# Forming three of every four blocks of the MLP's first matrix product from seven block products instead of eight

## The chip, the cores and the metric

The kernel runs on one NeuronCore of one Trainium2 chip. The metric is the device time of one execution in microseconds (us), lower is better. Three runs of the kernel before gave 1271.30, 1271.11 and 1271.58 us, so the median is 1271.3 us.

## What is computed

A two-layer encoder over 528 tokens (16 learned meta tokens and 512 inputs) with 1024 features. Layer 0 is an mLSTM mixer, layer 1 a differential attention; each is followed by a squared-ReLU MLP. Only the two MLPs change. Cut to what matters, the reference has:

```
def sq_relu_mlp(y, w_up, w_down):          # w_up 1024 x 4096, w_down 4096 x 1024
    u = y @ w_up
    return jnp.square(jax.nn.relu(u)) @ w_down

h = h + sq_relu_mlp(rmsnorm(h, norm_gains[i, 1]), mlp_w_up[i], mlp_w_down[i])
```

Layer 0 computes all 528 tokens, layer 1's MLP only the 512 that are put out.

## The kernel before

**Layout.** Features lie on the 128 partitions and tokens along the free axis: `h`, `yh`, `yl`, `ah`, `al` are tiles of 8 feature blocks by 528 tokens. Every matrix product is done in fp32r with a high and a low part of each side: `x = xh + xl`, and the product is `wh*yh + wh*yl + wl*yh`, three matmuls in place of one. ScalarE makes the high part by a copy that rounds (`wh<-raw`, line 513), VectorE the low part by a subtraction (`wl<-raw,wh`, line 885).

**Units.** The MLP works in units of 128 output features. A unit multiplies a 1024x128 strip of weights with all tokens: 8 blocks of the contraction times 3 matmuls times the token spans. In layer 0 there are two spans of 264 tokens (48 matmuls of 264 columns a unit), in layer 1 one of 512 (24 matmuls of 512 columns). Two neighbouring units share one DMA of weights (1 MB) and are called a row pair here. A group is 8 units of the first matrix ("up", 4 row pairs) and then 8 units of the second ("down", 4 row pairs) that use the 8 activation blocks just made; each layer has 4 groups, so 16 up pairs and 16 down pairs. Groups 1 to 3 run in loops of the engines' own.

**Around a unit.** After an up unit VectorE takes the positive part out of PSUM and multiplies by the token's norm factor (`tbuf<-ps,rb`, line 1105). ScalarE squares it twice: in full precision into `abuf` (line 708) and rounded into `ah` (line 709). VectorE makes `al<-abuf,ah` (line 1110). A down unit starts with block 0 of `ah`/`al` and waits, block by block, for `a_ready` (which `al` counts up). After a down unit VectorE adds PSUM to `h` (line 1083). SyncE issues the weight DMAs into two raw slots, each as soon as both units in a slot are split. GpSimd has nothing in the MLP but the masks for layer 1's attention (`qm`, `khm`, lines 499 and 500), which PE's first score products (line 1531) wait for.

**What sets the order.** Each engine has one queue in program order; semaphores tie them together. On VectorE an iteration of an up unit is: split a later unit's weights, then lines 1105 and 1110. PE's unit waits for its weights (`split_lo`) and for its PSUM banks (`evac`). The few lines on which the rest hangs:

```
for kb in range(kb0, kb1):
    ...
    for n, (w, m) in enumerate(((wh, mh), (wh, ml), (wl, mh))):
        for s, (t0, w_) in enumerate(spans):
            last = mm(ps[:, bank + s, 0:w_], w[:, slot, kb, :], m[:, kb, t0:t0 + w_],
```

## Time and profile before

| | before |
|---|---|
| median of 3 runs | 1271.3 us |
| the profiled execution's own time | 1271.11 us |
| its span, first to last instruction | 1269.4 us |
| granted TensorE clock, mean | 0.995 of 2.4 GHz |
| PE busy | 1239.7 us (98%), 8261 matmuls |
| VectorE busy | 696.9 us (55%) |
| ScalarE busy | 574.3 us (45%) |

Busy time of PE is the union of overlapping matmuls, whose ends are modelled; how long one really takes is read from start to start. An engine's idle time costs nothing unless another one waits for what it does next. The profiled execution took 1271.11 us, 1.7 us more than its span.

### The profile page before, as it was taken

What the parts mean: (1) busy time and instruction counts of PE and PEld (TensorE: products, weight loads), DVE (VectorE), ACT (ScalarE), POOL (GpSimd) and SP (SyncE); (2) the same over time, 40 slices, a digit from 0 to 9 for tenths busy, and PEclk for the clock granted to TensorE, in tenths of its full rate; (3) what the DMA queues carried; (4) which work ended last, traced back from release to release, by engine and by line L of the source; (5) the groups of instructions that cost most, each with busy time, mean ns of one, the idle gap of its engine ahead of it and who ended that gap; (6) DMA issues with size and microseconds to landing.
All of it is one profiled execution on the core that took longest, in us unless ns stands there. A gap on an engine that the chain in (4) does not pass through costs nothing.

```text
span 1269.4 us, 20753 instructions
## 1 busy us (share of the span) xinstructions
PE 1239.7 (98%) x8261; PEld 1137.4 (90%) x8261; DVE 696.9 (55%) x1026; ACT 574.3 (45%) x975; POOL 65.6 (5%) x105
## 2 busy tenths in 40 slices
PE   7999999999999999999999999998999999999997
PEld 6999999999999999999998998886788888888886
DVE  5778777754334334334558888785543442443443
ACT  4676776533224124123346787775431231331342
POOL 4121120110000000000010000000000000000000
PEclk9899999999999999999999999999999999999998
DMA  6433332222233222322222122212333322223311
GB/s 161 105 91 95 83 98 77 87 85 88 84 96 100 86 81 99 98 67 99 83 67 84 51 66 66 83 34 70 97 100 100 100 100 91 74 99 99 100 67 67
DMA packets 141575, 110.29 MB, mean 87 GB/s; under 512 B 22104, under 2 KB 139920, under 8 KB 141520
## 3 DMA queue, kind: packets, MB, share of 16 engines
q1 hardware_dynamic: 140000, 104.93, 27.0%
q0 software_dynamic: 1392, 4.49, 1.4%
q8 instruction: 39, 0.64, 0.2%
q14 instruction: 16, 0.13, 0.0%
q10 hardware_dynamic: 128, 0.09, 0.0%
HBM read 107.38 MB, written 2.13 MB: 86 GB/s over the span
## 4 chain that ended last, share of the span: by engine, by line
PE 76%; issue 18%; DVE 2%; ACT 2%; POOL 1%; DMA 1%; SPq 0%; DVEq 0%; POOLq 0%; ACTq 0%
PE ps L1313 72%; PE ps L1363 1%; PE ps L1381 1%; DMA raw<-in_mlstm_w_in_dram 1%; ACT wh L513 0%; PE ps L1404 0%; DVE wl L885 0%; PE ps L1416 0%; PE ps L1437 0%; PE ps L1470 0%; PE ps L1329 0%; POOL acc L430 0%; DVE fin L1295 0%; DVE yl L927 0%; POOL sql L506 0%
## 5 line engine op out<-in xcount | busy, mean ns | idle before, releaser
L1313 PE MATMUL ps<-yh,wh 128*128 128x264 f32 (+1 forms) x1472 | 366.5, 312 | 0.0
L1313 PE MATMUL ps<-yl,wh 128*128 128x264 f32 (+1 forms) x1472 | 361.9, 309 | 0.0
L1313 PE MATMUL ps<-yh,wl 128*128 128x264 f32 (+1 forms) x1472 | 360.9, 309 | 0.0
L513 ACT ACTIVATE wh<-raw 128x1024 fp32r<-128x1024 f32 x192 | 200.3, 1050 | 185.5 <-PE ps L1313 184.7
L1313 PE MATMUL ps<-ah,wh 128*128 128x264 f32 (+1 forms) x960 | 257.4, 322 | 1.6 <-DVE al L1284 0.8
L1313 PE MATMUL ps<-al,wh 128*128 128x264 f32 (+1 forms) x960 | 257.1, 322 | 0.0
L1313 PE MATMUL ps<-ah,wl 128*128 128x264 f32 (+1 forms) x960 | 256.4, 321 | 0.0
L1313 PEld LDWEIGHTS ps<-yh,wh 128*128 128x128 f32 x1472 | 240.2, 189 | 14.1 <-issue 0.2
L1313 PEld LDWEIGHTS ps<-yh,wl 128*128 128x128 f32 x1472 | 239.3, 189 | 13.8
L885 DVE TENSOR_TENSOR wl<-raw,wh 128x1024 fp32r<-128x1024 f32 x192 | 236.7, 1233 | 26.7 <-ACT wh L513 23.7
L1313 PEld LDWEIGHTS ps<-yl,wh 128*128 128x128 f32 x1472 | 239.3, 189 | 12.9 <-issue 0.2
L1313 PEld LDWEIGHTS ps<-ah,wh 128*128 128x128 f32 x960 | 159.7, 188 | 17.1 <-DVE al L1284 1.2
L1083 DVE TENSOR_TENSOR h<-ps,h 128x528 f32<-128x528 f32 (+1 forms) x80 | 55.9, 699 | 212.0 <-PE ps L1313 212.0
L1313 PEld LDWEIGHTS ps<-ah,wl 128*128 128x128 f32 x960 | 159.4, 188 | 13.7
L1313 PEld LDWEIGHTS ps<-al,wh 128*128 128x128 f32 x960 | 159.4, 188 | 13.3
L708 ACT ACTIVATE abuf<-tbuf 128x528 f32<-128x528 f32 (+1 forms) x64 | 40.9, 638 | 267.3 <-DVEq L1108 267.3
L1105 DVE SCALAR_TENSOR_TENSOR tbuf<-ps,rb 128x528 f32<-128x528 f32 (+1 forms) x64 | 44.8, 700 | 113.0 <-PE ps L1313 107.3
L1110 DVE TENSOR_TENSOR al<-abuf,ah 128x528 fp32r<-128x528 f32 (+1 forms) x64 | 44.8, 701 | 82.6 <-ACT ah L709 82.6
L513 ACT ACTIVATE yh<-h,gains 128x528 fp32r<-128x528 f32 (+1 forms) x32 | 23.4, 730 | 60.9 <-DVEq L1088 55.2
L709 ACT ACTIVATE ah<-tbuf 128x528 fp32r<-128x528 f32 (+1 forms) x64 | 39.9, 623 | 0.0
L759 ACT ACTIVATE e<-ps,stat 128x272 f32<-128x272 f32 (+3 forms) x48 | 26.5, 556 | 19.9 <-DVE stat L1168 18.4
L460 POOL TENSOR_SCALAR_AFFINE_SELECT dmat<-dmat 128x128 f32<-128x128 f32 (+1 forms) x40 | 19.2, 512 | 138.4 <-ACT dmat L587 138.4
(220 smaller groups left out, 1068.9 us busy)
## 6 DMA issues: line engine op xcount, KB each, us to landing
raw<-in_mlp_w_up_dram SPq DMA_DIRECT2D x32, 1024.0 KB, 5.3
raw<-in_mlp_w_down_dram SPq DMA_DIRECT2D x32, 1024.0 KB, 4.9
raw<-in_diff_w_in_dram SPq DMA_DIRECT2D x24, 512.0 KB, 3.7
raw<-in_mlstm_w_in_dram SPq DMA_DIRECT2D x16, 512.0 KB, 4.2
raw<-in_mlstm_w_in_dram SPq DMA_DIRECT2D x16, 256.0 KB, 5.4
raw<-in_mlstm_w_out_dram SPq DMA_DIRECT2D x3, 1024.0 KB, 5.0
raw<-in_diff_w_out_dram SPq DMA_DIRECT2D x3, 1024.0 KB, 4.9
mbc<-gate_rows POOLq DMA_DIRECT2D x8, 264.0 KB, 5.4
```

The source lines that it names most:

```text
L460: last = nc.gpsimd.affine_select(out=blk, in_=blk, compare_op=ALU.is_ge, fill=0.0, base=0, pattern=[[1, w]], channel_multiplier=-1)
L513: return nc.scalar.activation(o, i, ACT.Copy, scale=scale)
L708: nc.scalar.activation(abuf[:, t0:T], tbuf[:, t0:T], ACT.Square).then_inc(sqa_done, 1)
L709: nc.scalar.activation(ah[:, k, t0:T], tbuf[:, t0:T], ACT.Square).then_inc(ah_done, 1)
L759: nc.scalar.activation(dst, src, ACT.Exp, bias=stat[:, i % 2, c:c + 1], accum_out=stat[:, i % 2, 2 + c:3 + c]).then_inc(exp_done[c], 1)
L885: V.tensor_tensor(wl[:, k, :, :], raw[:, k // 2, :, P * (k % 2):P * (k % 2) + P], wh[:, k, :, :].bitcast(F32), ALU.subtract).then_inc(spli ...
L1083: ins = V.tensor_tensor(tokens(h[:, b, :], spans), src or banks(k, spans), tokens(h[:, b, :], spans), ALU.add)
L1105: V.scalar_tensor_tensor(tokens(tbuf[:, :], spans), banks(k, spans), 0.0, tokens(rb[:, :], spans), ALU.max, ALU.mult).then_inc(evac, 1)
L1110: V.tensor_tensor(al[:, k, t0:T], abuf[:, t0:T], ah[:, k, t0:T].bitcast(F32), ALU.subtract).then_inc(a_ready, 1)
L1313: last = mm(ps[:, bank + s, 0:w_], w[:, slot, kb, :], m[:, kb, t0:t0 + w_], start=(kb == 0 and n == 0), stop=(kb == CB - 1 and n == 2))
L1363: last = mm(ps[:, b, c:c + t1 - t0], what(rows, j), p, start=(b not in seen), stop=(n in (1, len(PIECES) - 1) and i == len(passes) - 1))
L1381: last = mm(ps[0:rows, b, c:c + t1 - t0], ks[par][:, s0:s0 + rows], q[:, t0:t1], start=(m == 0), stop=(m == 1))
```

## The change

In groups 1 to 3 of each layer every up pair is computed by block products after Winograd's form of Strassen's scheme; group 0's four up pairs and all down pairs stay as they were (called plain). For such a pair ("crossed" in the code) the weights are a 2x2 of blocks: two halves of the contraction (512 rows each) by two units (128 columns each). The tokens are two halves: 264 and 264 in layer 0, 256 and 256 in layer 1. Eight half-size products become seven, named A11, A12, S2, S3, S1, S4, A22. Each is 4 blocks of the contraction times 3 matmuls: 12 matmuls of 264 or 256 columns. What is added for it:

- VectorE makes four combined weight blocks (`form`: S1, S3, S2, S4, each 512 columns wide, into `lof`), and the low parts of all seven (`form_lo`, `natural_lo`). ScalarE makes the high parts.
- VectorE adds the products up in seven steps (`total`: C11, U2, U3, C22, U4, C12, C21), each 264 or 256 columns with one operand in PSUM. ScalarE copies A11 out of PSUM first (`snap`).
- The norm factor can't be put on afterwards, so the normed input itself is made once a layer: `scaled_y` (8 operations), `y_forms` (4 combined inputs, 8 operations), `forms_lo` (4 of 4x264 columns) and `scaled_lo` (4 of 2x528), with ScalarE's `forms_hi` and `scaled_hi`. They stand in the queues at up pairs 0 to 3 and at pair 4.
- The positive part squared is made in one VectorE pass (`square`: max(x,0) times x), and ScalarE only copies it into `ah`. Plain pairs keep two squares on ScalarE.
- All MLP loops are written out. Weights lie in two halves of SBUF, one a pair; the masks on GpSimd and VectorE move from before layer 0's MLP to its last down pairs and its end.

Cut to its core (`i` is the pair, 0 to 31 in a layer; `m` the unit in it; `after` is true if pair i+2 is crossed):

```diff
+            def total(i, name):
...
+                    if name == "C11":
+                        dve.wait_ge(m_done, items + DONE[i, "A12"])
+                        dve.wait_ge(t1_done, ranks + RANK[i])
...
+                        o, x, y = tb[0][:, first], t1[:, 0:w], p("A12")
...
+                    V.tensor_tensor(o, x, y, ALU.add).then_inc(c_done, 1)
...
+                def square(i, m):
...
+                    V.scalar_tensor_tensor(ab[m][:, t0:T], tb[m][:, t0:T], 0.0, tb[m][:, t0:T], ALU.max, ALU.mult).then_inc(m_relu, 1)
...
+                def form(i, name, after):
...
+                    a11, a12, a21, a22 = r[:, 0:4, 0:P], r[:, 4:8, 0:P], r[:, 0:4, P:2 * P], r[:, 4:8, P:2 * P]
...
+                    x, y, op = {"S1": (a21, a22, ALU.add), "S3": (a11, a21, ALU.subtract),
+                                "S2": (f[:, 16:20, :], a11, ALU.subtract), "S4": (a12, f[:, 8:12, :], ALU.subtract)}[name]
...
+                    dve.wait_ge(m_done, items + last_use(i, name))
+                    V.tensor_tensor(f[:, out_rows, :], x, y, op).then_inc(s_made, 1)
...
+                for i in range(PAIRS):
...
+                    if crossed(i - 1):
+                        total(i - 1, "C21")
+                    elif i > 0:
+                        evacuate(i - 1, 1)
+                    if crossed(i - 1):
+                        act_lo(i - 1, 0)
+                    if crossed(i + 1):
+                        form_lo(i + 1, "S23")
+                    if crossed(i - 1):
+                        square(i - 1, 1)
+                    if crossed(i):
+                        total(i, "C11")
+                    if crossed(i + 1):
+                        form_lo(i + 1, "S14")
+                    if crossed(i):
+                        total(i, "U2")
+                    if is_up(i - 1):
+                        act_lo(i - 1, 1)
+                    if crossed(i + 1):
+                        natural_lo(i + 1, False)
+                    elif 1 <= i < PAIRS - 1:
+                        plain_lo(layer, i + 1, 1)
+                    if crossed(i):
+                        total(i, "U3")
...
+                    if not crossed(i):
+                        evacuate(i, 0)
+                        if is_up(i):
+                            if i < 2:
+                                scaled_y(4 * i)
+                            act_lo(i, 0)
+                            if i == 2:
+                                for n in range(4):
+                                    y_forms(n)
+                            if i == 3:
+                                for n in range(4):
+                                    forms_lo(n)
...
+                    after = crossed(i + 2)
+                    if after:
+                        natural_lo(i + 2, True)
+                    elif i + 2 < PAIRS:
+                        plain_lo(layer, i + 2, 0)
...
+                    if crossed(i):
+                        total(i, "C22")
+                        total(i, "U4")
+                    if after:
+                        form(i + 2, "S1", 0)
+                        form(i + 2, "S3", 0)
+                    if crossed(i):
+                        total(i, "C12")
+                    if after:
+                        form(i + 2, "S2", 1)
+                    if crossed(i):
+                        square(i, 0)
+                    if after:
+                        form(i + 2, "S4", 3)
...
+                def plain(i, m):
...
+                        if not is_up(i) and i % 8 == 4 and m == 0:
+                            pe.wait_ge(a_ready, 8 * (4 * layer + i // 8) + kb + 1)
...
+                def product(i, name):
+
+                    n = 7 * (i % 8) + PRODUCTS.index(name)
+                    bank = n % 8
...
+                    if n >= 8:
+
+                        last, product_ = i - i % 8 + (n - 8) // 7, PRODUCTS[(n - 8) % 7]
+                        if product_ == "A11":
+                            pe.wait_ge(t1_done, ranks + RANK[last])
+                        else:
+                            pe.wait_ge(c_done, 7 * ranks + summed(last, FREED[product_]))
...
+                        for n, (x, y) in enumerate(((hi, mh), (hi, ml), (lo, mh))):
+                            last = mm(ps[:, bank, 0:w], x[1 - i % 2][:, row + kb, :], y,
+                                      start=(kb == 0 and n == 0), stop=(kb == 3 and n == 2))
```

PE before, at an up unit of layer 0 in the groups' loop; `wh`, `wl` are the weights' parts, `yh`, `yl` the input's, and each row is two matmuls with the same weights on the two halves of the tokens:

```order
L1313 MATMUL ps<-yh,wh 128x264 x2
L1313 MATMUL ps<-yl,wh 128x264 x2
L1313 MATMUL ps<-yh,wl 128x264 x2
L1305 REGISTER_ALU
L1313 MATMUL ps<-yh,wh 128x264 x2
```

PE now, at product S2 of the second crossed pair (pair 9 of layer 0); `hi`, `lo` are the weights' parts, `th`, `tl` those of the combined input:

```order
L1947 MATMUL ps<-yh,lo_107 128x264
L1947 MATMUL ps<-th,hi_106 128x264 [waits c_done,m_lo]
L1947 MATMUL ps<-tl,hi_106 128x264
L1947 MATMUL ps<-th,lo_107 128x264
L1947 MATMUL ps<-th,hi_106 128x264
```

A matmul now stands alone on its weights, no longer in twos, and a product waits for the sum that frees its bank (`c_done`) besides its weights (`m_lo`).

VectorE before, for one up unit (layer 0's first and second):

```order
L885 TENSOR_TENSOR wl<-raw,wh 128x1024 [waits split_hi]
L1105 SCALAR_TENSOR_TENSOR tbuf<-ps,rb 128x528 [waits unit_done,rb_ready]
L1110 TENSOR_TENSOR al<-abuf,ah 128x528 [waits evac,ah_done]
L885 TENSOR_TENSOR wl<-raw,wh 128x1024 [waits split_hi]
L1105 SCALAR_TENSOR_TENSOR tbuf<-ps,rb 128x528 [waits unit_done]
L1110 TENSOR_TENSOR al<-abuf,ah 128x528 [waits evac,ah_done]
```

VectorE now, from C21 of pair 8 (the first row) to U3 of pair 9 and the next pair's weights; `u`, `t` and `tbuf` hold the sums, `lof` the combined weights:

```order
L1375 TENSOR_TENSOR tbuf_115<-u_113,ps 128x264 [waits c_done,m_done]
L1387 TENSOR_TENSOR al<-abuf,ah 128x528 [waits ah_done]
L1327 TENSOR_TENSOR lo_110<-lof_111,hi_109 128x1024 [waits m_hi,s_made]
L1381 SCALAR_TENSOR_TENSOR abuf_116<-tbuf_115 128x528 [waits ah_done,c_done]
L1375 TENSOR_TENSOR tbuf<-t_117,ps 128x264 [waits ah_done,m_relu,t1_done,m_done]
L1327 TENSOR_TENSOR lo_110<-lof_111,hi_109 128x1024 [waits m_hi,s_made]
L1375 TENSOR_TENSOR u_112<-t_117,ps 128x264 [waits c_done,m_done]
L1387 TENSOR_TENSOR al<-abuf_116,ah 128x528 [waits ah_done]
L1334 TENSOR_TENSOR lo_110<-raw,hi_109 128x512 [waits m_hi]
L1375 TENSOR_TENSOR u_113<-u_112,ps 128x264 [waits c_done,m_done]
L1334 TENSOR_TENSOR lo_107<-raw,hi_106 128x1024 [waits m_hi]
```

In place of 6 operations for a pair VectorE now has 20, the sums taken in between the making of the next two pairs' weights.

VectorE now, behind the evacuation of pair 2's first unit up to the last activation block of group 0 (`tf` are the combined inputs, `tl` their low parts, `tbuf<-ps,rb` the evacuations of units (2,1), (3,0) and (3,1)):

```order
L1436 TENSOR_TENSOR tf<-yn_121,tf 128x528
L1287 TENSOR_TENSOR lo_110<-raw,hi_109 128x1024 [waits m_hi]
L1397 SCALAR_TENSOR_TENSOR tbuf_115<-ps,rb 128x528 [waits ah_done,m_done]
L1387 TENSOR_TENSOR al<-abuf_116,ah 128x528 [waits ah_done]
L1287 TENSOR_TENSOR lo_110<-raw,hi_109 128x1024 [waits m_hi]
L1397 SCALAR_TENSOR_TENSOR tbuf<-ps,rb 128x528 [waits ah_done,m_done]
L1387 TENSOR_TENSOR al<-abuf,ah 128x528 [waits ah_done]
L1449 TENSOR_TENSOR tl<-tf,th 128x1056 [waits t_made,th_done] x4
L1287 TENSOR_TENSOR lo_107<-raw,hi_106 128x1024 [waits m_hi]
L1397 SCALAR_TENSOR_TENSOR tbuf_115<-ps,rb 128x528 [waits ah_done,m_done]
L1387 TENSOR_TENSOR al<-abuf_116,ah 128x528 [waits ah_done]
```

Eight operations on `tf` (the last is shown) and four on `tl` now stand ahead of the evacuations in VectorE's queue, where before each unit had its own three alone.

## Rows read from the trace of the kernel before

**Rows 1.** The page: span and busy engines.

```profile
span 1269.4 us, 20753 instructions
PE 1239.7 (98%) x8261; PEld 1137.4 (90%) x8261; DVE 696.9 (55%) x1026; ACT 574.3 (45%) x975; POOL 65.6 (5%) x105
```

**Rows 2.** The chain, in order of time (start us, us, what): both MLPs.

```profile
274.56 370.04 PE ps L1313 x3024
...
906.31 322.49 PE ps L1313 x1392
```

**Rows 3.** Windows in the two MLPs: us, busy (x count), PEclk, DMA share, GB/s.

```profile
278.00:635.00 357.00, 357.00 (x2920) 357.00 (x2920) 145.60 (x165) 104.57 (x136) 0.00 (x0) 1.00 0.28 90
910.00:1225.00 315.00, 315.00 (x1362) 255.36 (x1361) 129.63 (x148) 94.13 (x123) 0.00 (x0) 1.00 0.29 95
```

**Rows 4.** Timeline of PE in an mLSTM head (start us, us, what).

```profile
102.22 0.28 PE L1363 MATMUL ps<-phi,vh 128*128 128x256 f32 x1
102.34 0.28 PE L1363 MATMUL ps<-plo,vh 128*128 128x256 f32 x1
...
102.57 0.23 PE L1363 MATMUL ps<-phi,vh 128*128 128x128 f32 x1
...
103.57 0.33 PE L1363 MATMUL ps<-phi,vh 128*128 128x272 f32 x1
103.74 0.29 PE L1363 MATMUL ps<-plo,vh 128*128 128x272 f32 x1
```

**Rows 5.** Weight loads, by line of the page.

```profile
L1313 PEld LDWEIGHTS ps<-yh,wh 128*128 128x128 f32 x1472 | 240.2, 189 | 14.1 <-issue 0.2
```

**Rows 6.** Timeline of VectorE in an mLSTM head.

```profile
114.99 0.42 DVE L1046 SCALAR_TENSOR_TENSOR acc<-acc,ps 128x256 f32<-128x256 f32 x1 [0.33 <-PE ps L1416]
115.33 0.43 DVE L1048 SCALAR_TENSOR_TENSOR acc<-acc,ps 128x272 f32<-128x272 f32 x1
115.68 1.22 DVE L885 TENSOR_TENSOR wl<-raw,wh 128x1024 fp32r<-128x1024 f32 x1
116.81 0.70 DVE L1056 SCALAR_TENSOR_TENSOR acc<-acc,of 128x528 f32<-128x528 f32 x1
117.92 0.71 DVE L904 TENSOR_TENSOR of<-ps,rb 128x528 f32<-128x528 f32 x1 [0.40 <-PE ps L1313]
118.54 0.70 DVE L1066 TENSOR_TENSOR nf<-nf,acc 128x528 f32<-128x528 f32 x1
119.24 0.69 DVE L1070 TENSOR_TENSOR vl<-ps,vh 128x512 fp32r<-128x512 f32 x1
119.84 0.27 DVE L1072 TENSOR_TENSOR vl<-ps,vh 16x128 fp32r<-16x128 f32 x1
```

**Rows 7.** Timeline of VectorE at an up unit of layer 0, then layer 1.

```profile
280.47 0.71 DVE L1105 SCALAR_TENSOR_TENSOR tbuf<-ps,rb 128x528 f32<-128x528 f32 x1 [0.27 <-PE ps L1313]
282.49 0.71 DVE L1110 TENSOR_TENSOR al<-abuf,ah 128x528 fp32r<-128x528 f32 x1 [1.31 <-ACT ah L709]
283.44 1.23 DVE L885 TENSOR_TENSOR wl<-raw,wh 128x1024 fp32r<-128x1024 f32 x1 [0.24 <-ACT wh L513]
...
907.73 0.69 DVE L1105 SCALAR_TENSOR_TENSOR tbuf<-ps,rb 128x512 f32<-128x512 f32 x1 [3.57 <-ACT rb L551]
909.70 0.69 DVE L1110 TENSOR_TENSOR al<-abuf,ah 128x512 fp32r<-128x512 f32 x1 [1.28 <-ACT ah L709]
```

**Rows 8.** Timeline of ScalarE at the same up unit of layer 0.

```profile
281.82 0.63 ACT L709 ACTIVATE ah<-tbuf 128x528 fp32r<-128x528 f32 x1
282.36 1.04 ACT L513 ACTIVATE wh<-raw 128x1024 fp32r<-128x1024 f32 x1
```

**Rows 9.** Activations' blocks, and what PE's down units waited, by line of the page.

```profile
L1313 PE MATMUL ps<-ah,wh 128*128 128x264 f32 (+1 forms) x960 | 257.4, 322 | 1.6 <-DVE al L1284 0.8
```

**Rows 10.** Timelines of GpSimd and PE: masks, and the first score products.

```profile
646.45 1.10 POOL L500 CAST khm<-kmask 64x528 fp32r<-64x528 f32 x1
...
663.66 0.30 PE L1531 MATMUL ps<-khm,qm 128*128 128x144 f32 x1 [0.89 <-DVE vf L904]
```

More of the change, by code:

```diff
@@ L61, with is_up, crossed, pe_order @@
 AHEAD = 2
-MISSED = [(7, 6), (14, 12)]
 CAME = [(0, 0, 0), (9, 9, 8)]
-U_IN0, U_OUT0, U_MLP0 = 0, 24, 32
-U_IN1, U_OUT1, U_MLP1 = 96, 120, 128
-U_END = 192
+U_IN0, U_OUT0 = 0, 24
+U_IN1, U_OUT1 = 32, 56
+U_END = 64
+PLAIN = 8
+PAIRS = 8 * GROUPS
+def is_up(i):
+    return 0 <= i < PAIRS and i % 8 < 4
+def crossed(i):
+    return is_up(i) and i >= PLAIN
+PRODUCTS = ("A11", "A12", "S2", "S3", "S1", "S4", "A22")
+def pe_order():
+    for i in range(PAIRS):
+        yield from [(i, e) for e in (PRODUCTS if crossed(i) else (0, 1))]
+def counted(things):
+    return {x: n + 1 for n, x in enumerate(things)}
+DONE = counted(pe_order())
+READY = counted((i, e) for i in range(PAIRS) for e in (("A1", "S23", "S14", "A22") if crossed(i) else (0, 1)))
+PLAINS = counted((i, m) for i in range(PAIRS) if not crossed(i) for m in range(2))
+RANK = counted(i for i in range(PAIRS) if crossed(i))
+N_DONE, N_READY, N_PLAIN, N_CROSSED = (len(x) for x in (DONE, READY, PLAINS, RANK))
+SUMS = {"C11": 1, "U2": 2, "U3": 3, "C22": 4, "U4": 5, "C12": 6, "C21": 7}
+FREED = {"A12": "C11", "S2": "U2", "S3": "U3", "S1": "U4", "S4": "C12", "A22": "C21"}
+SLOT = {"A11": 0, "A12": 1, "S2": 2, "S3": 3, "S1": 4, "S4": 5, "A22": 6}
+FORM = {"S1": 0, "S2": 1, "S3": 2, "A22": 3}
+UP_BANKS = [(0, 2, 4, 6, 0, 2, 4, 6), (4, 5, 7, 6, 4, 5, 7, 6)]
+def bank_of(i, name):
+    return (7 * (i % 8) + PRODUCTS.index(name)) % 8
+def summed(i, sum_):
+    return 7 * (RANK[i] - 1) + SUMS[sum_]
 ALL = [(0, HALF), (HALF, HALF)]
@@ L392, in _ @@
             out_weights(w_out0, U_OUT0)
-            mlp(0, U_MLP0)
-            with sp.Fori(0, HEADS) as i:
+            mlp(0)
+            for j in range(3):
+                sp.wait_ge(m_lo, READY[PAIRS - 2 + j // 2, 1])
+                sp.dma_start(raw[:, j // 2, :, P * (j % 2):P * (j % 2) + P], columns(w_in1, D * j, P)).then_inc(unit_in[j], 16)
+            with sp.Fori(1, HEADS) as i:
                 for j in range(3):
@@ L1151, in _ @@
             dve.wait_ge(lam_dve, 4)
+            mlp(0, ALL)
+            split(U_IN1 + 2, 2)
             dve.wait_ge(mask_base, 3)
@@ L1490, in _ @@
                 blocks(U_OUT0 + k, k % 4, ah, al, ALL, 2 * (k % 4), U_OUT0 + k - 3)
-            def mlp(layer, base, spans):
-                g0 = 4 * layer
-                def group(u0, g, first=False):
-                    for k in range(8):
-                        unit(u0 + k, k, yh, yl, spans, y_block(2 * layer + 1) if first and k == 0 else None)
-                        if first and k == 0:
-                            mean_squares(2 * layer + 1, spans)
-                    for k in range(8):
-                        unit(u0 + (8 + k), k, ah, al, spans,
-                             (lambda kb: pe.wait_ge(a_ready, g * 8 + (kb + 1))) if k == 0 else None)
-                group(base, g0, True)
-                with pe.Fori(1, GROUPS - layer) as g:
-                    group(g * 16 + base, g + g0)
```

478 lines of the change are left out of this document (366 added, 112 removed).

## The prediction

> **What bounds the kernel now.** I read the page first: PE is busy 98% of the span, VectorE 55%, ScalarE 45% [rows 1]. Then the chain in order of time: each MLP is one unbroken piece on PE, 3024 matmuls in 370.04 us in layer 0 and 1392 in 322.49 us in layer 1 [rows 2]. So a matmul of 264 columns takes 0.1224 us from start to start and one of 512 columns 0.2317 us. The windows confirm that no one else sets the pace there: PE fills 357.00 of 357.00 us and 315.00 of 315.00 us at clock 1.00 (the 2.4 GHz level), VectorE is busy 145.60 and 129.63 us, ScalarE less [rows 3]. In the MLPs, then, time is matmuls times their spacing, and whatever is added on VectorE costs nothing until PE waits for it.
>
> **What the change takes from PE.** Layer 0: a crossed pair goes from 2 units x 48 = 96 matmuls to 7 x 12 = 84, all of 264 columns. 12 matmuls x 0.1224 = 1.469 us a pair, 12 pairs: **17.6 us**. Layer 1: 48 matmuls of 512 columns become 84 of 256. For these I need the spacing of 256-column matmuls with their own weights each; four starts in an mLSTM head, 102.22, 102.34, (102.45) and 102.57, give 0.35 us for three, 0.117 us [rows 4]. 48 x 0.2317 = 11.12 us against 84 x 0.1175 = 9.87 us, 1.25 us a pair, 12 pairs: **15.0 us**. Bounds: the spacing can't be above that of 264 columns with equal loads (0.1224: 10.1 us gained) unless the weight load shows, and 0.117 gives 15.5. Together 32.6 us (27.7 to 33.1). Down pairs, heads and DMA bytes stay the same.
>
> **What it adds on VectorE.** Durations are one thing, spacing another: after a 528-column operation at 117.92 the next starts at 118.54, 0.62 us later though the first lasts 0.71; 512 columns 0.60, 272 columns 0.35, 256 columns 0.34, 1024 columns 1.13 [rows 6]. The order now shows 20 operations a crossed pair: 7 sums (0.34), 2 squares and 2 `al` (0.62), 4 forms and one half split (0.60), 3 of 1024 columns (1.13): 2.4 + 2.5 + 3.0 + 3.4 = **11.3 us** against PE's 84 x 0.1224 = 10.28 (9.87 in layer 1). For these pairs VectorE is the longer one. But only pairs 8 and 9 of a group carry all of it: pair 10 makes no further forms (8.9 us), pair 11 neither and splits plain weights (7.2 us). Walked through the queue: VectorE enters pair 8 some 1.3 us late (form S4 of pair 9 must wait until unit (7,1) has let go of its weights), is 2.4 to 2.7 us late after pair 8, about 3.7 after pair 9 at the most, about 2.3 after pair 10, and has caught up within pair 11.
>
> Is this lateness covered? A product waits for the sum that frees its bank eight products back: S2 of pair 9 for C11 of pair 8, which is due a whole pair, 9.9 to 10.3 us, earlier. The weights of pair i+1 are split in pair i, 7 us or more ahead of use. So 3.7 us is hidden by PE's own next pair. If that cover is gone, each us beyond it is paid once a group. The next in line is the end of pair 11: `al` of the last block. From A22's end: 0.05 to start, C21 0.34, `al` of block 6 0.62, square 0.71, ScalarE's copy 0.63 (its length by the `ah` row, [rows 8]) with two hand-overs of 0.04, `al` 0.71: 3.1 to 3.2 us. PE's down unit comes to its block 7 after 7 x 6 x 0.1224 = 5.14 us (layer 1: 7 x 3 x 0.2317 = 4.87). 1.7 us to spare, nothing paid. ScalarE has 3 x 1.04 + 2 x 0.63 and, by the same slope, about 0.6 and 0.4 for the half copy and A11: 5.4 us a pair, no limit.
>
> **Where I expect a wait: pair 3 to pair 4 of group 0.** Eight y-forms and four `tl` operations stand ahead of evacuations there, and each evacuation needs its round through ScalarE. VectorE's queue from the evacuation of (2,0): evacuation to `al` 2.0 (282.49 - 280.47, [rows 7]), `al` 0.62, y-forms 8 x 0.62 + 0.1, split 1.13, evacuation (2,1) to `al` 2.0, `al` to the split behind ScalarE's copy 0.95 (283.44 - 282.49), split 1.13, evacuation (3,0) to `al` 2.0, 0.98 to the first `tl`, 4 x 1.17, split 1.13, evacuation (3,1) to `al` 2.0, `al` and hand-over 0.75: 24.4 us. PE in the same time: three units of 5.87 us and 5.14 us up to block 7, less 0.05: 22.7. **1.7 us** of wait. Layer 1: 4 x 1.97 + 0.60 + 4.9 + 3 x 1.13 + 2 x 0.95 + 4 x 1.13 + 0.73 = 23.9 against 3 x 5.56 + 4.87 - 0.05 = 21.5: **2.4 us**. Together 4.1 us (0 if VectorE catches up earlier, up to 8 if each hand-over takes 0.1 more). Before, all the waits of PE's down units came to 1.6 us [rows 9], so this one is new. `scaled_lo` at pair 4 (4 x 1.17) comes after it and PE needs it only at pair 8.
>
> **At nothing.** The masks: 0.8 us on VectorE and eight copies of up to 1.1 us on GpSimd now begin about 5.5 us after layer 0's MLP ends, done at most 14 us after it; the first score product came 19 us after that end (663.66 against 644.6, [rows 10, 2]). SyncE's waits are those of two splits ago, as before; each load has over half a pair of time. The written-out loops: the unbroken piece of layer 0 holds the unlooped first group and the looped ones alike, at one spacing [rows 2].
>
> **Sum.** 1271.1 (this execution's time) - 32.6 + 4.1 = **1242.6 us**. The median of the runs shown lies 0.2 above that execution, which changes nothing. PE's waits end in a clock question only if they get long; I take the clock as it is.
>
> **Rivals.**
>
> 1. *All hidden*: no wait at pair 4, because VectorE starts evacuations earlier than in my walk. 1271.1 - 32.6 = 1238.5. For it: 1.7 and 2.4 us are differences of sums of 24. Against: the walk leaves nothing idle on VectorE but the rounds through ScalarE.
>
> 2. *VectorE's operations don't overlap*, each takes its whole duration: 0.43, 0.71, 0.69 and 1.23 [rows 6, 7] make 13.0 us a pair, and VectorE is 1.3 + 2 x 2.7 = 6.7 us late after two pairs, 4.7 at the end of pair 11 (10.2 and 8.3 us of work in the last two). `al` of block 7 comes 3.1 + 4.7 = 7.8 us into the down unit: 2.7 us a group, in layer 1 some 4.1; six groups 20.4, the y-chain 2.2 more: 1265. Half of it gives 1254. For it: 20 operations with two or three waits each, many on the operation shortly before. Against: the rows just quoted, where an operation starts 0.09 before the last ends. The Trainium skill, "VectorE: DVE Perf Modes", section "The DRAIN you can't avoid", says that the next operation does not start until the pipe is empty. By that rule this rival would be the forecast; the trace disagrees for operations that don't wait (0.62 spacing at 0.71 duration).
>
> 3. *Slower, by VectorE as the bound*: if besides full durations each of the 20 operations waits 0.1 us for its partner, a group's four pairs take 44.4 + 8 = 52.4 us on VectorE against 41.1 on PE; with 1.3 late at the start and 2.0 to spare that is 10.6 us a group, 64 in all: 1306. It turns the gain into a loss from 4.8 us a group on, that is at 46.6 us of work in four pairs, against 38.7 at spacings. Against: the waits are mostly for things long done.
>
> 4. *Slower, by weight loads that show*: each 256-column matmul brings its own load, whose row shows 0.189 us [rows 5]. In an mLSTM head a 272-column matmul behind narrow ones took 0.17 us (103.57 to 103.74, [rows 4]). If all 84 did: 14.3 us a pair, 2.5 and 3.2 us more than before, 12 pairs each: 68 + 4 = 1343. It loses from 0.132 us a matmul on in layer 1. Against: at 264 columns the same load is there for every matmul, at 0.1224. The Trainium skill, "TensorE: Matmul & The Clock Gate", section "Part 3: Packing small matmuls", lets a load overlap running matmuls only when the row group differs; the 0.117 of the rows at 256 columns disagrees with it.
>
> **How the numbers follow.** My forecast (1239.5 to 1247) 0.55; all hidden 0.14; VectorE's lateness partly or wholly paid (1247 to 1265) 0.25; slower by VectorE 0.04; slower by loads 0.02. The range of 8 in 10 takes in the first two and rival 2 to a bit over its half: 1238 to 1257. 0.2% of 1271 is 2.5 us, about what can be told from no change here. Faster 0.94, same 0.01, slower 0.05.
>
> **What the new profile would show.** PE 8261 - 4608 + 4896 = 8549 matmuls; 1008 of them of 264 columns and 1008 of 256 in products, at 0.122 and 0.1175; VectorE busy some 200 us more (24 x 6.6 and two y-chains of about 20), the 20 operations a pair at 11 to 12 us; PE waiting at `ps<-ah,hi` for `al` once a layer at pair 4, about 2 us, and not at pairs 12, 20, 28. Wrong if waits stand at each group's first down pair (rival 2), inside pairs 9 to 11 for `c_done` (rival 3), or if the 256-column spacing is over 0.125 (rival 4).

## The result, and the profile after

The changed kernel takes 1242.75 us (median of 4 executions, 1241.34 to 1244.20); the kernel before took 1271.23 us on the same chip. The ratio is 0.9776, 95% interval 0.9759 to 0.9793. The forecast was 1242.6 us, the range 1238 to 1257. The profiled execution was the longest of the four, 1244.20 us, with a span of 1242.1 us, 27.3 us shorter than before.

The page of the changed kernel (compare [rows 1]: 8549 matmuls, as forecast, and 190 us more on VectorE, where some 200 were forecast):

```profile
span 1242.1 us, 21698 instructions
PE 1208.6 (97%) x8549; PEld 1129.8 (91%) x8549; DVE 887.2 (71%) x1386; ACT 608.2 (49%) x1015; POOL 62.0 (5%) x105
L1911 PE MATMUL ps<-ah,hi 128*128 128x264 f32 (+1 forms) x768 | 206.2, 323 | 3.8 <-DVE al L1387 3.8
```

The last row answers to [rows 9]: PE's waits for activation blocks rose from 1.6 to 3.8 us. L1911 is the line of plain matmuls now, L1947 that of the block products. The chain of the changed kernel in order of time (start us, us, what) answers to [rows 2]:

```profile
322.57 41.92 PE ps L1911 x342
364.49 40.77 PE ps L1947 x336
405.25 46.76 PE ps L1911 x384
452.01 40.77 PE ps L1947 x336
...
976.43 39.69 PE ps L1947 x336
1016.12 44.63 PE ps L1911 x192
```

The single unbroken piece of each MLP is now cut at product lines, with no idle time between the pieces shown. Four crossed pairs take 40.77 us in layer 0 (0.1213 us a matmul of 264 columns) and 39.69 us in layer 1 (0.1181 us of 256). In layer 0 they took 384 x 0.1224 = 47.0 us before, in layer 1 192 x 0.2317 = 44.5 us: 6.2 and 4.8 us less a group, three groups each. Four plain pairs take 46.76 us (0.24 less than before) and 44.63 us (0.14 more).

The piece of layer 0 is broken once, at pair 4 of group 0, and that of layer 1 at the same place. Timeline of PE there in the changed kernel (start us, us, what, and in brackets the idle time and its releaser):

```profile
320.50 0.40 PE L1911 MATMUL ps<-ah,lo 128*128 128x264 f32 x2
322.57 0.51 PE L1911 MATMUL ps<-ah,hi 128*128 128x264 f32 x2 [1.66 <-DVE al L1387]
...
932.26 0.39 PE L1911 MATMUL ps<-ah,lo 128*128 128x512 f32 x1
934.84 0.50 PE L1911 MATMUL ps<-ah,hi 128*128 128x512 f32 x1 [2.18 <-DVE al L1387]
...
935.98 0.63 PE L1911 MATMUL ps<-al,hi 128*128 128x512 f32 x1
936.40 0.63 PE L1911 MATMUL ps<-ah,lo 128*128 128x512 f32 x1
```

From start to start PE stood 1.8 us beyond the usual spacing in layer 0, and 2.3 us in layer 1. Behind the second wait something else is to be seen: soon the matmuls lie 0.42 us apart (935.98 to 936.40) instead of 0.233. The windows of the changed kernel around both waits say why (us, busy and count of PE, PEld, DVE, ACT, POOL, then PEclk, DMA share, GB/s):

```profile
316.00:326.00 10.00, 8.34 (x69) 8.13 (x68) 8.52 (x10) 7.29 (x9) 0.00 (x0) 1.00 0.08 18
932.00:942.00 10.00, 7.82 (x27) 5.89 (x26) 8.53 (x10) 6.83 (x8) 0.00 (x0) 0.83 0.31 105
```

The granted clock is 1.00 around the first wait and 0.83 around the second: about a third of those 10 us was granted at half speed, 1.2 GHz. Those are 3.4 us, and they cost half of that, 1.7 us.

So the account of the two spans is: block products 18.7 + 14.4 = 33.1 gained, plain pairs 20 x 0.06 - 20 x 0.035 = 0.5 gained, waits 4.1 and clock 1.7 lost. That leaves 27.8 gained where 27.3 is measured.

### The profile page after: what moved, and what is told of

It is laid out like the page before. It is cut to its first block, busy times and chain, and to the rows that moved or that the text cites. A ratio compares the mean times of both kernels' runs of the same rounds, so it can differ in the third digit from the quotient of the medians.

```text
span 1242.1 us, 21698 instructions
## 1 busy us (share of the span) xinstructions
PE 1208.6 (97%) x8549; PEld 1129.8 (91%) x8549; DVE 887.2 (71%) x1386; ACT 608.2 (49%) x1015; POOL 62.0 (5%) x105
## 4 chain that ended last, share of the span: by engine, by line
PE 72%; issue 19%; DVE 6%; ACT 3%; POOL 1%; DMA 0%; DVEq 0%; POOLq 0%; ACTq 0%
PE ps L1911 33%; PE ps L1947 19%; PE ps L1691 15%; PE ps L1741 1%; PE ps L1759 1%; DVE wl L1079 1%; DVE tf L1436 1%; ACT wh L627 0%; DVE tbuf L1397 0%; ACT ah L862 0%; DVE tl L1449 0%; DVE lo L1287 0%; DMA meta_in<-in_meta_tokens_dram 0%; PE ps L1782 0%; DVE yl L1121 0%
## 5 line engine op out<-in xcount | busy, mean ns | idle before, releaser
L1911 PE MATMUL ps<-ah,hi 128*128 128x264 f32 (+1 forms) x768 | 206.2, 323 | 3.8 <-DVE al L1387 3.8
L1911 PE MATMUL ps<-al,hi 128*128 128x264 f32 (+1 forms) x768 | 206.0, 323 | 0.0
L1911 PE MATMUL ps<-ah,lo 128*128 128x264 f32 (+1 forms) x768 | 205.3, 321 | 0.0
L1691 PE MATMUL ps<-yh,wh 128*128 128x264 f32 (+1 forms) x704 | 161.2, 303 | 0.4 <-DVE wl L1079 0.4
L1691 PE MATMUL ps<-yl,wh 128*128 128x264 f32 (+1 forms) x704 | 156.1, 296 | 0.0
L1691 PE MATMUL ps<-yh,wl 128*128 128x264 f32 (+1 forms) x704 | 156.0, 296 | 0.0
L1911 PEld LDWEIGHTS ps<-ah,hi 128*128 128x128 f32 x768 | 127.7, 189 | 15.9 <-DVE al L1387 4.5
L1911 PEld LDWEIGHTS ps<-ah,lo 128*128 128x128 f32 x768 | 127.8, 189 | 11.3
L1911 PEld LDWEIGHTS ps<-al,hi 128*128 128x128 f32 x768 | 127.8, 188 | 11.2
L1691 PEld LDWEIGHTS ps<-yh,wh 128*128 128x128 f32 x704 | 112.4, 190 | 3.0 <-DVE wl L1079 0.7
L1947 PE MATMUL ps<-th,hi 128*128 128x264 f32 (+1 forms) x384 | 108.5, 283 | 0.0
L1947 PE MATMUL ps<-tl,hi 128*128 128x264 f32 (+1 forms) x384 | 108.3, 282 | 0.0
L1947 PE MATMUL ps<-th,lo 128*128 128x264 f32 (+1 forms) x384 | 108.2, 282 | 0.0
L1079 DVE TENSOR_TENSOR wl<-raw,wh 128x1024 fp32r<-128x1024 f32 x64 | 80.5, 1259 | 8.1 <-ACT wh L627 6.2
L1947 PE MATMUL ps<-yh,lo 128*128 128x264 f32 (+1 forms) x288 | 81.3, 282 | 0.0
L1947 PE MATMUL ps<-yh,hi 128*128 128x264 f32 (+1 forms) x288 | 81.3, 282 | 0.0
```

The lines of the kernel that those rows point to most:

```text
L1079: V.tensor_tensor(wl[:, k, :, :], raw[:, k // 2, :, P * (k % 2):P * (k % 2) + P], wh[:, k, :, :].bitcast(F32), ALU.subtract).then_inc(spli ...
L1911: last = mm(ps[:, b + s, 0:cw], x[half][:, 20 * m + kb, :], y[:, kb, c0:c0 + cw], start=(kb == 0 and n == 0), stop=(kb == CB - 1 and n == 2))
L1947: last = mm(ps[:, bank, 0:w], x[1 - i % 2][:, row + kb, :], y, start=(kb == 0 and n == 0), stop=(kb == 3 and n == 2))
```

## Experiments

All are the changed kernel with one edit. An edit ahead of a line moves its number: the plain matmuls are L1911 or L1916 below, `al` L1387 or L1392. Each ratio is to the kernel before on the same chip.

**The changed kernel once more.**

> The changed kernel once more, unchanged, to see whether the half-clock stretch behind layer 1's wait of 2.3 us comes in every execution. If the four times seen so far (1241.3 to 1244.2) differ by whether it came: a profile without it has a span near 1240.4, one with it 1242.1, layer 1's pair 4 taking 13.5 us or 15.2. If it comes always, the spread has another cause.

It took 1243.0 us (1241.24 to 1244.53, 5 executions; ratio 0.9782, 0.9768 to 0.9795). The wait at pair 4 of layer 1 and the 3.4 us at half clock behind it came again at the same place (the two profiled executions, 1244.20 and 1244.28 us, are among the longest, so this doesn't say that every execution has them). A single execution moves by 3 us, and longer ones have a lower mean clock (0.993 at 1244.3 and 1244.5 us, 0.996 at 1241.2), so differences under 2 us are read from the traces below, not from medians.

**The low and high parts of the combined inputs two pairs later.**

ScalarE's part first, then VectorE's, which moves from the up pair 3 to the down pair 5:

```diff
-                    if i == 3:
+                    if i == 5:
                         for n in range(4):
                             forms_hi(n)
...
-                            if i == 3:
-                                for n in range(4):
-                                    forms_lo(n)
...
+                        elif i == 5:
+                            for n in range(4):
+                                forms_lo(n)
```

> The rounding and the low parts of the four combined inputs (forms_hi, forms_lo) move from up pair 3 to down pair 5; nothing else changes. Theory A (the wait of PE at pair 4 is VectorE's queue: 4.7 us of tl operations stand ahead of the last evacuation of group 0): the queue is 4 x 1.17 + 1.0 us shorter, which is more than the 1.9 and 2.3 us waited, so both waits go, and with them the stretch at half clock behind layer 1's: 4.2 + 1.7 us less than the changed kernel, 1237 to 1238.5 us. Theory B (the wait comes from ScalarE's rounds of the evacuations, not from the tl operations in the queue): over 1 us of wait stays at pair 4. Theory C (pair 5's VectorE work then delays a down pair): a new wait at pair 6 or 7 and no gain.

It took 1237.54 us (1237.12 to 1239.74; ratio 0.9745, 0.9731 to 0.9758), 5.2 us below the changed kernel. Its chain in order of time:

```profile
273.72 87.65 PE ps L1911 x720
361.37 40.77 PE ps L1947 x336
...
885.74 83.71 PE ps L1911 x360
969.45 39.69 PE ps L1947 x336
```

Both cuts are gone: 720 and 360 plain matmuls run through without a break. 83.71 / 360 = 0.2325 us, so no part of them ran at half clock either. What was given back is 1.8 + 2.3 + 1.7 = 5.8 us by the trace, 5.2 by the medians. (The spans differ by 6.9 us, 1.2 of it ahead of the first MLP, where this edit isn't.) This ties the wait to the four `tl` operations and their ScalarE partners in front of pair 3's last evacuation; the two were moved together, so their shares aren't told apart. It was put in the forecast as the price of the change; it is the price of the place.

**Half of them later.**

Forms 0 and 1 stay at pair 3, forms 2 and 3 go to pair 5, on ScalarE alike:

```diff
                             if i == 3:
-                                for n in range(4):
+                                for n in range(2):
                                     forms_lo(n)
...
+                        elif i == 5:
+                            for n in range(2, 4):
+                                forms_lo(n)
```

> Only half of these operations (the last two of four, high and low parts) moves to pair 5. Theory A: the queue up to the last activation block of group 0 is 2 x 1.17 us shorter in layer 0 and 2 x 1.14 in layer 1. Layer 0's wait of 1.9 goes wholly, layer 1's 2.3 falls to 0 to 0.2; the clock does not fall. 1237 to 1239 us. Theory B: more than 1 us of the wait stays in each layer.

It took 1237.19 us (1236.88 to 1239.71; ratio 0.9744, 0.9729 to 0.9759), no different from the version above. Layer 0's wait is gone, and 0.08 us of layer 1's is left. These two are the fastest versions of this study, 0.4% below the changed kernel.

**The combined inputs' first eight operations twice.**

```diff
+                        V.tensor_tensor(tf[:, f, o, 0:w], x, y, ALU.subtract).then_inc(pad_done, 1)
+                        padded[0] += 1
+                        dve.wait_ge(pad_done, padded[0])
                         V.tensor_tensor(tf[:, f, o, 0:w], x, y, ALU.subtract).then_inc(t_made, 1)
```

> Each of the eight y-forms at pair 2 is computed twice, each extra one waited for: 8 x 0.73 = 5.8 us more in VectorE's queue in layer 0, 8 x 0.71 = 5.7 in layer 1, nothing on PE. Theory A: nothing of it is hidden, since the queue has no slack left up to pair 4: PE waits 7.7 and 8.0 us there in place of 1.9 and 2.3, and the clock falls to half behind both. 1242.8 + 11.5 + 1.7 to 4 = 1256 to 1258 us. Theory B (VectorE has slack behind pair 2 that the forecast's walk did not see): under 8 us more.

It took 1253.96 us (1253.03 to 1257.09; ratio 0.9873, 0.9858 to 0.9889), 11.2 more. PE's waits in the whole execution, by releaser (us in total, times, longest), begin with:

```profile
PE ps L1915 <- DVE tbuf L1398: 8.0, 2, 4.1
...
PE ps L1915 <- DVE al L1388: 2.9, 2, 1.9
```

Read from start to start the four waits are 4.1 and 2.1 us in layer 0, 4.3 and 1.2 in layer 1: 11.7 in place of 4.1, which is 4 us less than the queue was made longer by. The rest is clock. It fell at three of these waits:

```profile
313.50:316.90 3.40, 3.40 (x18) 3.40 (x17) 2.53 (x3) 1.49 (x3) 0.00 (x0) 0.50 0.05 7
327.10:330.50 3.40, 3.40 (x16) 3.40 (x17) 3.09 (x4) 3.40 (x5) 0.00 (x0) 0.51 0.23 67
931.30:938.10 6.80, 5.68 (x14) 4.51 (x14) 4.11 (x6) 3.90 (x6) 0.00 (x0) 0.50 0.15 50
```

In layer 1 it fell 1.1 us before PE started again (932.42). PE lost some 6.3 us by it in place of 1.7. The longer queue first stops PE at pair 3 for a PSUM bank (`tbuf` frees it), the clock falls behind that wait, and PE comes to the last activation block of group 0 later, so that it waits less there. VectorE's queue from `al` of pair 2's first unit to that block's `al` shows that none of the added work was hidden. First the changed kernel, then this one:

```profile
300.25 0.71 DVE L1387 TENSOR_TENSOR al<-abuf,ah 128x528 fp32r<-128x528 f32 x1 [1.25 <-ACT ah L862]
...
321.81 0.71 DVE L1387 TENSOR_TENSOR al<-abuf,ah 128x528 fp32r<-128x528 f32 x1 [1.24 <-ACT ah L862]
```

```profile
298.75 0.71 DVE L1388 TENSOR_TENSOR al<-abuf,ah 128x528 fp32r<-128x528 f32 x1 [1.25 <-ACT ah L863]
...
326.25 0.71 DVE L1388 TENSOR_TENSOR al<-abuf,ah 128x528 fp32r<-128x528 f32 x1 [1.24 <-ACT ah L863]
```

21.56 us became 27.50: 5.9 more, for eight operations 0.74 apart. PE's start behind the wait for that block is 5.9 us later in layer 0 and 5.8 in layer 1, counted from the start of each MLP's second unit. So each microsecond of queue cost PE one microsecond, part of it as a wait and part as half clock between two waits. Only a half-clock stretch behind the last wait comes on top: layer 0 has one here (327.10) and layer 1 has lost its own. That is why the time is below the 1256 to 1258 us expected, though nothing was hidden.

**One addition more in each crossed pair.**

```diff
+                    for _ in range(1 if name == "U2" else 0):
+                        V.tensor_tensor(o, x, y, ALU.add).then_inc(pad_done, 1)
+                        padded[0] += 1
+                        dve.wait_ge(pad_done, padded[0])
                     V.tensor_tensor(o, x, y, ALU.add).then_inc(c_done, 1)
```

> Every crossed pair gets one addition more on VectorE (the sum U2 is formed twice, one after the other, the second waiting for the first), about 0.45 us a pair, 1.8 us a group of four crossed pairs. Theory (spare time): VectorE's sums of a group may end 1.5 us later before PE waits for the last block's split form in the down pair, and VectorE is 2 us short of PE's time over the four pairs, so 1.8 us a group disappear: 1242 to 1244, no change to the changed kernel. Rival (VectorE has no slack left, since it is the longer one in pairs 8 and 9): each microsecond is paid, 6 groups x 1.8 = 11 us: 1253.

It took 1246.08 us (1244.82 to 1247.48; ratio 0.9801, 0.9785 to 0.9817): 3.3 more than the changed kernel, neither 0 nor 11. The two spans differ by 3.3 us as well. 1.3 of it arose ahead of the first MLP, where this edit isn't: this profile has half clock there that the changed kernel's hasn't (0.72 granted from 21 to 27 us). 0.7 arose elsewhere outside the waits. New waits for `al` make 1.3, from start to start: 0.2 us at the first down pair of each of layer 1's three groups, and 0.6 us at one of layer 0's three groups, the third. So the time to spare was as large as forecast within 0.2 us, and in one group smaller. Why there, the next but one experiment shows.

**Three additions more.** The same edit with `range(3 ...)`.

> The same with three additions more in every crossed pair: 5.4 us a group. Theory (spare time): lateness at the down pair becomes 0.3 + 38.8 + 5.4 - 40.8 = 3.7 us in layer 0 where 1.5 to 1.7 is free, so 2.2 us a group; in layer 1 4.1 against 1.5, 2.6 us a group; 3 x 4.8 = 14.4 us: 1257, and up to 10 more if PE's clock falls behind each of these waits. They stand at each group's first down pair, on PE's line of down products, released by the last `al`. Rival (no slack): 6 x 5.4 = 32 us, 1275, with the waits inside pairs 9 to 11 on VectorE's sums.

It took 1274.59 us (1273.44 to 1276.27; ratio 1.0031, 1.0019 to 1.0042): slower than the kernel before. The size is that of the rival, the place mostly that of the theory. Timeline of PE at a first down pair of layer 0:

```profile
407.71 0.41 PE L1916 MATMUL ps<-ah,lo 128*128 128x264 f32 x2
409.86 0.51 PE L1916 MATMUL ps<-ah,hi 128*128 128x264 f32 x2 [1.74 <-DVE al L1392]
...
411.90 0.51 PE L1916 MATMUL ps<-ah,hi 128*128 128x264 f32 x2 [1.05 <-DVE al L1392]
412.25 0.58 PE L1916 MATMUL ps<-al,hi 128*128 128x264 f32 x2
412.62 0.65 PE L1916 MATMUL ps<-ah,lo 128*128 128x264 f32 x2
```

PE waits for block 6 and again for block 7, 3.1 us together, and then runs at half clock (in the window 412.40 to 415.60 the granted clock is 0.50). Over six groups the waits for `al` come to some 17.6 us. Layer 1's groups add 0.4, 0.4 and 2.5 us at the start of the down pair for the sum that frees a PSUM bank, a wait that the theory didn't have: 20.9 us in all. The MLPs have 23.9 us at half clock in place of 3.4, in 1.8 us of which PE stood still anyway, so the clock costs some 9.3 us more. That makes 30.2 together, where the spans differ by 29.5 and the first MLP began 1.5 us earlier. Two terms of the expectation were short. The lateness at the down pair was 4.5 us, not 3.7: three chained additions take 1.4 us (0.46 each, not 0.45), and VectorE can't use its whole time, as its windows over the last three of the four pairs show in this kernel:

```profile
373.20:383.40 10.20, 10.20 (x86) 10.20 (x86) 9.93 (x18) 4.93 (x7) 0.00 (x0) 1.00 0.15 54
383.40:393.60 10.20, 10.20 (x86) 10.20 (x85) 9.95 (x18) 4.94 (x7) 0.00 (x0) 1.00 0.32 104
393.60:403.80 10.20, 10.20 (x86) 10.20 (x85) 9.55 (x20) 3.47 (x5) 0.00 (x0) 1.00 0.31 105
```

Even 4 us behind, VectorE stands 0.25 to 0.65 us a pair, for its round through ScalarE (`al` waits for `ah` 0.37 us at 399.81). The clock's part, "up to 10", came nearly in full.

**One addition more, and GpSimd's masks one pair later.**

```diff
-            pool.wait_ge(m_done, DONE[PAIRS - 5, "A22"])
+            pool.wait_ge(m_done, DONE[PAIRS - 4, 1])
```

> The kernel with one more addition a crossed pair, and GpSimd's seven mask operations of layer 0 (580.4 to 585.0 us in the changed kernel's trace, at the end of the third group) start one pair later, after the first down pair of the last group. In the changed kernel VectorE's square, `al` and split there take 1.11, 1.01 and 1.62 us in place of 0.71, 0.71 and 1.22. Theory (GpSimd's work beside it slows VectorE by 0.3 to 0.4 us an operation, and so uses up the time to spare in this group alone): PE's wait of 0.64 us at 586.5, seen with one more addition, goes, and the three operations take 0.71, 0.71 and 1.22 again; 0.5 us less than 1246.1. Rival (the third group is late by its own queue): the wait stays where it was.

It took 1245.18 us (1243.57 to 1245.35; ratio 0.9798, 0.9781 to 0.9814). The medians can't tell 0.5 us; the traces can. First the changed kernel at the end of pair 27, where the change has put the masks; the timeline of VectorE:

```profile
581.08 0.71 DVE L1387 TENSOR_TENSOR al<-abuf,ah 128x528 fp32r<-128x528 f32 x1 [0.31 <-ACT ah L627]
581.71 1.11 DVE L1381 SCALAR_TENSOR_TENSOR abuf<-tbuf 128x528 f32<-128x528 f32 x1
583.54 1.01 DVE L1387 TENSOR_TENSOR al<-abuf,ah 128x528 fp32r<-128x528 f32 x1 [0.71 <-ACT ah L627]
584.48 1.62 DVE L1287 TENSOR_TENSOR lo<-raw,hi 128x1024 fp32r<-128x1024 f32 x1
```

and GpSimd in the same time:

```profile
580.84 0.54 POOL L593 MEMSET kmask<- 64x528 f32 x1
581.63 0.63 POOL L598 TENSOR_SCALAR_AFFINE_SELECT qmask<-qmask 64x512 f32<-64x512 f32 x1
...
583.94 1.09 POOL L605 TENSOR_SCALAR_AFFINE_SELECT kmask<-kmask 64x528 f32<-64x528 f32 x1
```

Then VectorE in the kernel with the masks moved, at the same work:

```profile
582.47 0.71 DVE L1392 TENSOR_TENSOR al<-abuf,ah 128x528 fp32r<-128x528 f32 x1 [0.37 <-ACT ah L628]
583.09 0.70 DVE L1386 SCALAR_TENSOR_TENSOR abuf<-tbuf 128x528 f32<-128x528 f32 x1
584.50 0.71 DVE L1392 TENSOR_TENSOR al<-abuf,ah 128x528 fp32r<-128x528 f32 x1 [0.71 <-ACT ah L628]
585.46 1.23 DVE L1288 TENSOR_TENSOR lo<-raw,hi 128x1024 fp32r<-128x1024 f32 x1 [0.25 <-ACT hi L628]
```

The square, `al` and the split take 0.70, 0.71 and 1.23 us again where they took 1.11, 1.01 and 1.62, and PE's wait in the third group is gone. The theory holds: GpSimd's selections, which read and write SBUF, cost VectorE 0.3 to 0.4 us an operation. The `al` of 581.08, for most of its 0.71 us beside GpSimd's memsets (which only write), was not slowed. The Trainium skill, "SBUF — State Buffer", section "Who interferes with whom", says that a VectorE instruction with two SBUF inputs contends with a GpSimd instruction that reads SBUF, not with one that only writes; the trace agrees on both.

**The second square back on ScalarE.**

```diff
-                    V.scalar_tensor_tensor(ab[m][:, t0:T], tb[m][:, t0:T], 0.0, tb[m][:, t0:T], ALU.max, ALU.mult)
+                    V.tensor_scalar(tb[m][:, t0:T], tb[m][:, t0:T], 0.0, None, ALU.max)
-                        copy(ah[:, k, t0:T], ab[m][:, t0:T])
+                        nc.scalar.activation(ab[m][:, t0:T], tb[m][:, t0:T], ACT.Square)
+                        nc.scalar.activation(ah[:, k, t0:T], tb[m][:, t0:T], ACT.Square)
```

> Undoes the change's second part alone: the positive part of a crossed pair's two blocks is taken on VectorE without the square, and ScalarE makes both squares as it does in plain pairs. VectorE does the same count of operations of the same columns, ScalarE 2 x 0.6 us more a pair (6.6 of 10.2 us). One hand-over more lies between the relu and `al` of each block: ScalarE square, then square again, some 0.6 us later. Theory: PE is the bound and the `al` of block 7 then ends 4.3 us into the down pair where 5.14 (4.87) is needed, so no change: 1242 to 1244. Rival: the second square makes `al` late enough to be waited for, 6 x 0.5 to 1 us: 1246 to 1249.

It took 1244.51 us (1244.40 to 1244.84; ratio 0.9793, 0.9776 to 0.9809), 1.8 above the changed kernel's median and within its executions. In its trace PE waits 0.5 us in layer 0's third group and 0.3 us in each of layer 1's three, 1.4 in all. VectorE's single pass is thus worth 1.4 us by the trace. The edit isn't as clean as expected: the positive part alone takes VectorE 0.43 us where the square takes 0.71, and still the group's last `al` ended 4.7 us into the first down pair of layer 0, 1.0 later than in the changed kernel. These are waits for the group's last `al`, so what it shortens is the path from A22 to there; the operations that it leaves to ScalarE are not waited for elsewhere. In this profile the wait of 2.3 us at pair 4 of layer 1 had no half clock behind it.

**Product S2 in narrower matmuls.**

```diff
+                    for c0, cw in ((0, w // 2), (w // 2, w // 2)) if name == "S2" else ((0, w),):
...
-                                mh, ml = th[:, FORM[name], kb, 0:w], tl[:, FORM[name], kb, 0:w]
+                                mh, ml = th[:, FORM[name], kb, c0:c0 + cw], tl[:, FORM[name], kb, c0:c0 + cw]
...
-                            last = mm(ps[:, bank, 0:w], x[1 - i % 2][:, row + kb, :], y,
+                                last = mm(ps[:, bank, c0:c0 + cw], x[1 - i % 2][:, row + kb, :], y,
```

> On PE alone: product S2 of every crossed pair is made in two column halves, 24 matmuls of 132 (layer 1: 128) columns in place of 12 of 264 (256), with the same weights and sums. Theory A (a matmul with its own weights takes what its columns take, down to about 60 ns): no change, 1243. Theory B (the weight load is just hidden at 256 columns and shows below that, 0.109 us or so for the narrow matmuls): 24 x 0.109 - 12 x 0.12 = 1.2 us a pair, 24 pairs, 28 us: 1271. This tells how near the change is to the point at which the loads of its seven products would show.

It took 1272.94 us (1271.57 to 1273.55; ratio 1.0013, 1.0004 to 1.0023): the whole gain of the change is spent. Timeline of PE in a product S2:

```profile
365.68 0.22 PE L1948 MATMUL ps<-th,hi 128*128 128x132 f32 x1
365.74 0.27 PE L1948 MATMUL ps<-tl,hi 128*128 128x132 f32 x1
365.85 0.28 PE L1948 MATMUL ps<-th,lo 128*128 128x132 f32 x1
...
368.08 0.27 PE L1948 MATMUL ps<-tl,hi 128*128 128x132 f32 x1
```

From 365.74 to 368.08 lie 21 matmuls of 132 columns: 0.1115 us each, not 0.060. Half the columns cost 92% of the time. That this is the load and not a fixed price of each matmul is seen at the first narrow one, which took 0.06 us (365.68 to 365.74): beside the matmuls of 264 columns each load had started 0.12 us ahead of its matmul, from here on it is 0.06, and the loads themselves lie 0.11 us apart. The counts of [rows 1] and of the new page say that each matmul had a load of its own before the change too (8261 and 8261, now 8549 and 8549), also where two stand on the same weights. In this kernel's chain four crossed pairs take 45.70 and 44.83 us in place of 40.77 and 39.69, so 3 x 4.93 + 3 x 5.14 = 30.2 us, and 1242.75 + 30.2 is 1272.95. The Trainium skill, "TensorE: Matmul & The Clock Gate", section "LDWEIGHTS (loading the stationary operand)", has a load take its columns divided by 1.2 per ns, 107 ns for 128; the rows' 111.5 is 4% above that.

**The weight store laid out low parts first.**

```diff
-            hi.append(place(f"hi{half}", [P, 28, P], F32R, at, limit))
             lo_at = at[0]
             lo.append(place(f"lo{half}", [P, 28, P], F32R, at, limit))
             lof.append(place(f"lof{half}", [P, 28, P], F32, [lo_at], limit))
+            hi.append(place(f"hi{half}", [P, 28, P], F32R, at, limit))
```

> Only places in SBUF change: in both halves of the weight store the low parts are laid out first and the high parts behind them, in place of high first. Same instructions in the same order. Plain units of 48 matmuls of 264 columns in the changed kernel take 5.824, 5.840, 5.847 and 5.869 us (even pair first and second unit, odd pair first and second), the same in every group, where all took 5.873 before; in layer 1 5.599, 5.596, 5.576 and 5.563. Theory (how fast a weight load follows depends on where in SBUF it lies): the four lengths change by 10 ns or more, the time by 2 us at the most. Rival (it is the neighbourhood in the program, such as waits and semaphore updates between the matmuls): they stay within 3 ns.

It took 1243.37 us (1241.21 to 1245.74; ratio 0.9786, 0.9768 to 0.9804). The lengths of the plain units stayed what they were, 5.818 (5.830 for the first behind crossed pairs; the expectation's 5.824 is their mean), 5.840, 5.847 and 5.869 us in layer 0, within a nanosecond. This theory falls: exchanging the places of high and low parts isn't what sets them. Why 48 equal matmuls take 4 to 55 ns less than the 5.873 us of before, by the unit's place in two pairs and always the same, stays open; it is worth 1.2 us over 20 pairs of layer 0, and 0.7 the other way in layer 1.

## Why the prediction was right, step by step

- *What the change takes from PE.* Right: 32.6 forecast, 33.1 measured. The parts were off in opposite directions by about a microsecond: 264 columns at 0.1213, not 0.1224 (18.7 for 17.6), 256 columns at 0.1181, not 0.1175 (14.4 for 15.0).
- *What it adds on VectorE.* The spacings of [rows 6] were the right durations. (One spacing in them, 118.54 to 119.24 behind a 528-column operation, is 0.70, which the prediction passed over; nothing came of it.) The walk's lateness was up to 1 us too large: C21 of pairs 8, 9, 10 and 11 began 1.4, 2.7, 1.9 and 0.2 us behind the first matmul of the next pair, where 2.4 to 2.7, 3.7, 2.3 and 0 stood. The term at fault is pair 8: the walk had VectorE enter it 1.3 us late and pay the full 20 operations. In the trace it has fewer there (the window counts 15 where pairs 9 and 10 have 18), entered some 0.5 late and twice stood waiting for PE inside it (0.41 us each, before C11 and U3), so up to U3 it wasn't late at all. The changed kernel's VectorE windows over these four pairs show the rest:

```profile
364.32:374.53 10.21, 10.21 (x86) 10.21 (x85) 9.11 (x15) 2.81 (x4) 0.00 (x0) 1.00 0.33 100
374.53:384.70 10.17, 10.17 (x86) 10.17 (x85) 10.00 (x18) 4.94 (x7) 0.00 (x0) 1.00 0.16 46
384.70:394.92 10.22, 10.22 (x87) 10.22 (x85) 10.05 (x18) 4.94 (x7) 0.00 (x0) 1.00 0.21 68
394.92:405.09 10.17, 10.17 (x86) 10.17 (x85) 9.24 (x18) 3.47 (x5) 0.00 (x0) 1.00 0.49 157
```

  In pairs 9 and 10 VectorE is busy 98% and PE never waits: a whole pair of cover hides it.
- *Is this lateness covered?* Yes, with less to spare than forecast. The last `al` of the group, in VectorE's timeline of the changed kernel:

```profile
406.00 0.71 DVE L1387 TENSOR_TENSOR al<-abuf,ah 128x528 fp32r<-128x528 f32 x1 [0.28 <-ACT ah L627]
406.63 0.70 DVE L1381 SCALAR_TENSOR_TENSOR abuf<-tbuf 128x528 f32<-128x528 f32 x1
408.05 0.71 DVE L1387 TENSOR_TENSOR al<-abuf,ah 128x528 fp32r<-128x528 f32 x1 [0.71 <-ACT ah L627]
```

  It ends at 408.76, 3.7 us into the down pair that starts at 405.09; 3.1 to 3.2 was forecast, and 5.14 is needed. What was left out is the 0.2 us from the down pair's first matmul to C21 (A22's last matmul is shown to end 0.17 us into it) and `al` of block 6 waiting 0.28 for its own round. 1.5 us to spare in place of 1.7 to 2.0. The kernels with 1 and 3 additions more measured it: 1.8 us a group nearly vanish, 5.5 us a group cost more than 5.
- *The wait at pair 4.* Right in place, releaser and size: 1.7 and 2.4 forecast, 1.8 and 2.3 measured, and both go when the `tl` operations are moved. Rival 1 is refuted as an account of this kernel; at 1237.5 us it is what the moved version does.
- *"PE's waits end in a clock question only if they get long; I take the clock as it is."* This step failed by 1.7 us: 2.3 us can be long enough. That the total still came out within 0.2 us is luck: 1.7 lost here and 0.5 + 0.5 gained in the products and the plain pairs cancel in part, and the median of four lies 1.5 us below the profiled execution, which was itself 1.6 us above the forecast.
- *At nothing.* True of this kernel, but not because the masks were harmless. The prediction looked only at GpSimd's eight copies behind the MLP. GpSimd's mask operations that now run inside it slow three VectorE operations by 1.1 us together, hidden by the same 1.5 us to spare.
- *Rivals.* Rival 2 (VectorE's whole durations paid) did not happen: no waits at pairs 12, 20 and 28. The section of the Trainium skill that the prediction names there, "VectorE: DVE Perf Modes", "The DRAIN you can't avoid", goes on to say that a next operation that is not held starts earlier. So it doesn't disagree with the rows (0.62 apart at 0.71 us), and by it alone this rival wasn't the forecast. Rival 3, slower by VectorE as the bound, put its turning point at 4.8 us lost a group; three additions more passed it, at 31.8 us over six groups (5.3 each) and 1274.6 us. Rival 4, slower by weight loads, was nearer than its chance of 0.02 suggests: the spacing can't fall below 0.1115 us, and the products stand at 0.1181, 6% above this floor. At 256 columns the loads are hidden.
